# Query and key norm of a two-layer block: one chain of sums, roots and spread products made into two

## The reference

```
q = rms_norm(q, g_q) * (HEAD_DK ** -0.5)      # over each group of 64 channels
k = rms_norm(k, g_k)
bias = bias_table[t5_buckets(kpos[None, :] - qpos[:, None])]    # [q, k, head]
s = einsum('bqhjd,bkhjd->bhjqk', q, k) + bias
...
mod = dot(silu(c), w_mod) + b_mod              # shift1, scale1, gate1, shift2, scale2, gate2
x  = x + gate1 * mix
h2 = rms_norm(x, g_norm2) * (1.0 + scale2) + shift2
```

## Time and profile before

| | |
|---|---|
| median of 3 executions | 2403.66 us (2400.92 to 2405.05) |
| the profiled execution | 2396.91 us |
| its span in the trace | 2394.8 us |
| the block of the change | from 303.4 to 387.1 us of the span |
| PE busy | 2146.2 us (90% of the span) |
| DVE busy | 1744.9 us (73%) |
| ACT busy | 1053.7 us (44%) |
| POOL busy | 165.0 us (7%) |

### The profile page before, as it was taken

The page is one execution under the profiler, slowest core; times in us unless marked ns, Lnnn a source line. Parts: engine busy times, 40 slices in busy tenths (PEclk is TensorE's granted clock), DMA queues, the critical chain, the costliest instruction groups (busy, mean ns, idle before and its releaser), DMA issues. The chain is left out here.

```text
span 2394.8 us, 25614 instructions
## 1 busy us (share of the span) xinstructions
PE 2146.2 (90%) x10172; PEld 1667.9 (70%) x10172; DVE 1744.9 (73%) x1857; ACT 1053.7 (44%) x1190; POOL 165.0 (7%) x122
## 2 busy tenths in 40 slices
PE   5999979999954999999999069999999969899997
PEld 3767824667843888888887047888888647788775
DVE  4565135997467799999997359999999469955737
ACT  4387022774224677777775022112221246522123
POOL 2000000000000011111110000000000000042210
PEclk8999986999976999999999569999999978899999
DMA  9111170001276899999997311121222140332201
GB/s 316 44 36 36 36 286 0 1 1 72 88 277 254 316 403 394 395 393 403 393 393 245 127 44 38 63 79 36 83 102 88 33 153 1 124 114 88 71 1 71
DMA packets 125719, 365.03 MB, mean 152 GB/s; under 512 B 11733, under 2 KB 22893, under 8 KB 125623
## 3 DMA queue, kind: packets, MB, share of 16 engines
q1 hardware_dynamic: 111616, 328.68, 36.1%
q0 software_dynamic: 6336, 21.00, 3.4%
q10 hardware_dynamic: 7670, 14.03, 1.6%
HBM read 324.76 MB, written 38.86 MB: 152 GB/s over the span
## 5 line engine op out<-in xcount | busy, mean ns | idle before, releaser
L2031 DVE SCALAR_TENSOR_TENSOR arena<-arena,vecs 128x1023 f32<-128x1023 f32 (+14 forms) x240 | 304.4, 1268 | 7.1
L1560 DVE TENSOR_TENSOR w_low<-W,w_high 128x2048 fp32r<-128x2048 f32 x96 | 217.0, 2287 | 38.9 <-ACT w_high L1512 38.9
L1928 PE MATMUL Q<-hT_high,w_high 128*128 128x512 f32 (+1 forms) x736 | 227.0, 391 | 5.9 <-DVE ring_low L2074 5.8
L1560 DVE TENSOR_TENSOR w_low<-arena,w_high 128x2048 fp32r<-128x2048 f32 x96 | 218.3, 2290 | 17.7 <-ACT w_high L1512 17.7
L1512 ACT ACTIVATE w_high<-W 128x2048 fp32r<-128x2048 f32 x96 | 184.0, 1919 | 96.6 <-PE Q L1455 65.3
L1928 PE MATMUL Q<-hT_low,w_high 128*128 128x512 f32 (+1 forms) x720 | 222.2, 390 | 0.0
L1928 PE MATMUL Q<-hT_high,ring_low 128*128 128x512 f32 x704 | 217.2, 390 | 0.0
L1512 ACT ACTIVATE w_high<-arena 128x2048 fp32r<-128x2048 f32 x96 | 184.2, 1919 | 74.9 <-PE Q L1455 74.9
L1455 PE MATMUL Q<-w_high,x_high 128*128 128x512 f32 x512 | 160.8, 395 | 2.4 <-DVE x_low L1563 2.4
L1928 PEld LDWEIGHTS Q<-hT_high,w_high 128*128 128x128 f32 (+1 forms) x736 | 135.4, 184 | 39.0 <-DVE ring_low L2074 5.9
L1455 PE MATMUL Q<-w_low,x_high 128*128 128x512 f32 x512 | 158.8, 391 | 0.0
(11 more groups left out here) (430 smaller groups left out, 4295.1 us busy)
## 6 DMA issues: line engine op xcount, KB each, us to landing
W<-in_w_dram SPq DMA_DIRECT2D x48, 2048.0 KB, 13.3
arena<-in_w_dram SPq DMA_DIRECT2D x48, 2048.0 KB, 12.3
W<-in_w_mod_dram SPq DMA_DIRECT2D x12, 2048.0 KB, 9.5
W<-in_w_in_dram SPq DMA_DIRECT2D x12, 2048.0 KB, 8.7
W<-in_w_out_dram SPq DMA_DIRECT2D x6, 2048.0 KB, 9.0
spill<-arena ACTq DMA_DIRECT2D x24, 512.0 KB, 2.6
W<-in_w_in_dram SPq DMA_DIRECT2D x8, 1024.0 KB, 7.7
arena<-in_x_dram SPq DMA_DIRECT2D x4, 1024.0 KB, 17.4
```

The source lines that it names most:

```text
L1560: nc.vector.tensor_tensor(wl[:], chunk_src(r, j), wh[:].bitcast(F32), ALU.subtract).then_inc(low_v, 1)
L1928: ins = nc.tensor.matmul(Q[rows, 2 * (n % 4) + half, :], w[:, k], x[:, k, HALF * half:HALF * half + HALF], start=k == 0 and w is high and ...
L2031: ins = nc.vector.scalar_tensor_tensor(conf[:, i, j:], u[:, 0:S - j], w, conf[:, i, j:], ALU.mult, ALU.add)
```

## The change

- The norm is two chains, q (tiles 0 to 3) and k (tiles 4 to 7). Each has its 8 sums in its own rows (partitions 0 to 7 and 64 to 71) and PSUM pair, its own root, inversion and spread. The q chain's root and inversion stand in the lists between the sums of k.
- The inverse roots are split: ACT rounds them into rows 0 to 7 (64 to 71) of `qk_parts`, DVE puts the rest into rows 32 to 39 (96 to 103), the rows between are zero. `qk_spread` has the 0/1 matrix in both groups of rows, so one fp32r product over 40 rows spreads both parts. The spread uses two PSUM pairs in turn instead of four.
- `near` stands behind the first two sums and the first modulation vector. The bias transfers go from SP's list to POOL's; the weight units on SP follow the b_mod rows directly.
- The subtraction for the recurrent branch (`y_rest`, two instructions) goes to the end of DVE's list; the `gain2` load and the (1 + scale2) * g_norm2 step go to the output projection's block.

The diff, cut to its core:

```diff
-        VECS = 2 * 8
-        qk_sum = tiles(5)[:, 0:8 * VECS].rearrange("p (b r) -> p b r", b=8)
-        qk_spread = tiles(4)[0:VECS].rearrange("r (b p) -> r b p", b=8)
...
+        VECS = 2 * HEADS
+        qk_sum = tiles(5)[:, 0:HEADS * VECS].rearrange("p (b r) -> p b r", b=HEADS)
+        spread_whole = tiles(4)[:, 0:HALF]
+        qk_spread = rounded("qk_spread", 4, [P, 2, HEADS, P])[:, 1]
+        qk_parts = rounded("qk_parts", 3, [P, S])
+        sum_bank = (6, 2)
+        def rows_of(g):
+            return slice(DK * g, DK * g + VECS)
+        def rest_of(g):
+            return slice(DK * g + 32, DK * g + 32 + VECS)
...
-                sync.dma_start(gain2, bc_row(A["g_norm2"][0], D)).then_inc(gain2_in, 16)
...
-                for h in range(HEADS):
-                    sync.wait_ge(near_ready, h + 1)
-                    sync.dma_start(bias_rows[h].rearrange("(p n) -> p n", p=P), bias_near[h]).then_inc(bias_sent, 16)
-                sync.wait_ge(bias_sent, 16 * HEADS)
...
+                nc.gpsimd.memset(qk_parts[:].bitcast(F32), 0.0).then_inc(masks, 1)
+                for h in range(HEADS):
+                    pool.wait_ge(near_ready, h + 1)
+                    pool.dma_start(bias_rows[h].rearrange("(p n) -> p n", p=P), bias_near[h]).then_inc(bias_sent, 16)
+                pool.wait_ge(bias_sent, 16 * HEADS)
+                for h in range(HEADS):
+                    skewed = bias_rows[h, P:].rearrange("(p n) -> p n", n=HALF - 1)[:, 0:NEAR]
+                    pool.dma_start(bias_all[:, h, 6 * P:6 * P + NEAR], skewed).then_inc(bias_in, 16)
+                pool.wait_ge(bias_in, 16 * HEADS)
...
+                def next_vector(i):
+                    row_product(i)
+                    if i < 5:
+                        mod_product(pe, unit(pe, U_GATE1 + i + 1), 5)
+                def sums(g):
+                    for b in range(HEADS):
+                        n = HEADS * g + b
+                        pe.wait_ge(sq_ready, n + 1)
+                        for half in range(2):
+                            ins = nc.tensor.matmul(Q[rows_of(g), sum_bank[g] + half, :], qk_sum[:, b],
+                                                   tiles(n % 2)[:, HALF * half:HALF * half + HALF],
+                                                   start=b == 0, stop=b == HEADS - 1)
+                        ins.then_inc(sum_mm, 1)
+                        if b % 2:
+                            next_vector(2 * g + b // 2)
+                        if n == 1:
+                            near()
...
+                def spread(g):
+                    pe.wait_ge(parts_low, g + 1)
+                    span = slice(DK * g, DK * g + 32 + VECS)
+                    for b in range(HEADS):
+                        n = HEADS * g + b
+                        if n >= 2:
+                            pe.wait_ge(qk_normed, n - 1)
+                        for half in range(2):
+                            ins = nc.tensor.matmul(Q[:, 6 * (n % 2) + half, :], qk_spread[span, b],
+                                                   qk_parts[span, HALF * half:HALF * half + HALF],
+                                                   start=True, stop=True)
+                        ins.then_inc(spread_mm, 1)
...
                 mod_product(pe, unit(pe, U_GATE1), 5)
...
+                pe.wait_ge(masks, 2)
+                sums(0)
+                pe.wait_ge(near_ready, HEADS)
+                sums(1)
+                next_vector(4)
...
+                spread(0)
...
+                spread(1)
...
+                square(0)
+                square(1)
+                act.wait_ge(lam_mm, 1)
+                nc.scalar.activation(lam_pr[:, 2:4], Q[:, 4, 0:2], ACT.Exp).then_inc(lam_e, 1)
+                part(0)
+                square(2)
+                square(3)
+                act.wait_ge(masks, 6)
+                nc.scalar.activation(qk_spread, spread_whole.rearrange("r (b p) -> r b p", b=HEADS), ACT.Copy)\
+                    .then_inc(mask_ready, 1)
+                part(1)
+                root(0)
+                square(4)
+                square(5)
+                part(2)
+                square(6)
+                square(7)
+                act.wait_ge(masks, 7)
+                high_rows(0)
+                part(3)
+                root(1)
+                part(4)
...
+                part(5)
+                high_rows(1)
...
+                def invert(g):
+                    dve.wait_ge(root_q, g + 1)
+                    nc.vector.reciprocal(qk_rows[rows_of(g)], qk_rows[rows_of(g)]).then_inc(rows_inv, 1)
+                def low_rows(g):
+                    dve.wait_ge(parts_high, g + 1)
+                    nc.vector.tensor_tensor(qk_parts[rest_of(g)], qk_rows[rows_of(g)],
+                                            qk_parts[rows_of(g)].bitcast(F32), ALU.subtract).then_inc(parts_low, 1)
+                def norm(n):
+                    dve.wait_ge(spread_mm, n + 1)
+                    nc.vector.scalar_tensor_tensor(qk[:, n], qk[:, n], qk_gain[:, n // HEADS:n // HEADS + 1],
+                                                   bank2(3 * (n % 2)), ALU.mult, ALU.mult).then_inc(qk_normed, 1)
...
+                added(0)
+                for h in range(HEADS):
+                    dve.wait_ge(near_mm, h + 1)
+                    nc.vector.tensor_copy(bias_near[h], Q[:, h, :]).then_inc(near_ready, 1)
+                added(1)
+                invert(0)
+                added(2)
+                low_rows(0)
+                dve.wait_ge(near_ready, HEADS)
+                for h in range(HEADS):
+                    nc.vector.tensor_copy(bias_all[:, h, 0:6 * P], bias_near[h][:, 0:1].broadcast_to((P, 6 * P)))
+                    nc.vector.tensor_copy(bias_all[:, h, 6 * P + NEAR:],
+                                          bias_near[h][:, HALF - 1:HALF].broadcast_to((P, 6 * P)))
+                invert(1)
+                added(3)
+                added(4)
+                norm(0)
+                norm(1)
+                low_rows(1)
+                norm(2)
+                norm(3)
+                added(5)
+                for n in range(HEADS, 2 * HEADS):
+                    norm(n)
...
+                sync.dma_start(gain2, bc_row(A["g_norm2"][0], D)).then_inc(gain2_in, 16)
...
+                dve.wait_ge(gain2_in, 16)
+                nc.vector.scalar_tensor_tensor(SCALE2, SCALE2, 1.0, gain2, ALU.add, ALU.mult).then_inc(scale_made, 1)
```

More of the change, by code:

```diff
@@ L277, in program @@
         mod_rows = {4: GATE1, 6: SHIFT2, 8: SCALE2, 10: GATE2}
-        gain2 = tiles(3)
+        gain2 = tiles(2)
         GROUPS = 4
@@ L845, in row_product @@
                     nc.tensor.matmul(Q[:, 4, :], group_row, part_sb, start=True, stop=True).then_inc(row_mm, 1)
-                pe.wait_ge(masks, 3)
-                mod_product(pe, unit(pe, U_GATE1), 5)
-                for b in range(8):
-                    pe.wait_ge(sq_ready, b + 1)
-                    for half in range(2):
-                        ins = nc.tensor.matmul(Q[0:VECS, 6 + half, :], qk_sum[:, b],
-                                               tiles(b % 2)[:, HALF * half:HALF * half + HALF],
-                                               start=b == 0, stop=b == 7)
-                    ins.then_inc(sum_mm, 1)
-                    if b % 2:
-                        row_product(b // 2)
-                        mod_product(pe, unit(pe, U_GATE1 + b // 2 + 1), 5)
@@ new lines, in near @@
+                def near():
+                    pe.wait_ge(hot_in, 16)
+                    pe.wait_ge(table_ready, 1)
+                    for h in range(HEADS):
+                        nc.tensor.matmul(Q[:, h, :], table_bc[:, h], hot, start=True, stop=True).then_inc(near_mm, 1)
+                mod_product(pe, unit(pe, U_GATE1), 5)
+                pe.wait_ge(lam_ready, 1)
+                nc.tensor.matmul(Q[:, 4, 0:2], ones[0:DK, :], lam_pr[0:DK, 0:2], start=True, stop=True)\
+                    .then_inc(lam_mm, 1)
@@ L890, in _, with square, root @@
-                act.wait_ge(near_mm, HEADS)
+                def square(n):
+                    if n >= 2:
+                        act.wait_ge(sum_mm, n - 1)
+                    nc.scalar.activation(tiles(n % 2), qk[:, n], ACT.Square).then_inc(sq_ready, 1)
+                def root(g):
+                    act.wait_ge(sum_mm, HEADS * (g + 1))
+                    nc.scalar.activation(qk_rows[rows_of(g)],
+                                         Q[rows_of(g), sum_bank[g]:sum_bank[g] + 2, :].rearrange("p a b -> p (a b)"),
+                                         ACT.Sqrt, bias=eps_col[rows_of(g)], scale=1.0 / DK).then_inc(root_q, 1)
@@ new lines, in high_rows @@
+                def high_rows(g):
+                    act.wait_ge(rows_inv, g + 1)
+                    nc.scalar.activation(qk_parts[rows_of(g)], qk_rows[rows_of(g)], ACT.Copy).then_inc(parts_high, 1)
+                square(0)
[6 more added lines that the diff above has]
```

(8 more changed lines are left out.)

71 lines of the change are left out of this document (16 added, 55 removed).

## The result

| | median (executions) | range |
|---|---|---|
| before | 2403.12 us (4) | 2400.92 to 2405.05 |
| changed | 2376.90 us (4) | 2373.94 to 2381.78 |

The ratio is 0.9893, with a 95% interval of 0.9874 to 0.9912, so 26.2 us less. The forecast was 2382.5 us with a range of 2374.5 to 2390.0. The direction and the range held, and the gain was 5 us larger than the 21 of the forecast.

What follows compares the result with a forecast made beforehand. The block was taken as a serial piece of 83.7 us that nothing covers. Ending at 365.2 instead of 387.1 gives -21.9, the scale step +1.1, say -21: 2382.5 us from median 2403.66, range 2374.5 to 2390.0.

Steps and rivals of the forecast that it cites:

- The front: Block's start to the end of the eighth sum: work starts at 303.4 without waiting for one_hot, a gain of 9.8 us.
- T8: End of the eighth sum on PE in the block: 344.8 before, forecast 335, between 331.5 and 337.4.
- Root and fills: After the eighth sum, k's root takes 1.10 plus 0.3 to 336.4; q's fills end at 335.8, just hidden.
- The new gap on PE: PE idles some 5 us before row_product(4), waiting for added(3); low clock then: row product 1.9, modulation product 3.5.
- The first spread pair: First two rounded spread products after the modulation product: 0.9 plus 0.4 until DVE sees it, 1.3 us, to 350.3.
- DVE's row of norms to the end: Norms, low_rows, added(5) and subtractions on DVE, 13.9 us plus 1.0 of stalls, ending the block at 365.2.
- The tail: From the end of the eighth sum to the block's end: 42.3 us before, forecast 30.2.
- The moved scale step: (1 + scale2) * g_norm2, 1.23 us on DVE, delays the output projection's split and PE: charged at 1.1 us.
- the front gained more than forecast: Answers the first rival: late b_mod rows or a 1.2 GHz clock leave a gain of 15, 2389 us; chance 0.09.
- the spread is faster: Answers the second rival: fp32r products over 40 rows cost what float32 did, gain 4, 2400 us; chance 0.04.
- the bias chain on POOL: Third rival: POOL's bias transfers end the block last, at 377 if they take 60 us; gain 9, 2395; chance 0.03.
- the attention lost nothing: Answers the fourth rival: the clock stays down in the attention, 4.4 us lost a turn, eight turns 2418; chance 0.02.

Runs made afterwards that it cites:

- the two runs that began it at 2.4 GHz: Kernel before with its float32 spread over 128 rows, 2385.53 us; and the changed kernel with three steps moved plus nine unread float32 products, 2371.77 us.
- the one chain over 128 rows: Changed kernel with one 16-row norm chain, added(3) early, subtractions and scale step in DVE's gaps, rounded spread over 128 rows: 2371.01 us.
- the float32 spread: Changed kernel with plain float32 spread products over the 8 rows of a chain, without rounding or rest: 2390.49 us, block 69.9 us.
- the three moved steps run again: Changed kernel with added(3) before the second inversion, and subtractions and scale step in DVE's waits; second timing 2370.16 us, block 51.4 us.

## Why the prediction was right, and where it was off

Its steps, each by its own numbers:

- **The front.** Forecast T8 31.6 us after the start of the block, measured 30.2 (332.58 + 3.60 - 306.02). The b_mod rows landed 12.6 us after the start, as taken. What was off is the clock. It was taken half down over the front; the trace has 0.93. Near ran at full clock (3.88) and the price came one step later, in the sums behind it (5.07 instead of 3.60). The lower bound of 28.1 (T8 = 331.5) was not reached.
- **Root and fills.** The second inversion was to start within 2 us of T8 + 1; it started 1.8 after T8. The fills ended 0.7 us after the root: hidden, but only just.
- **The second inversion** is not hidden and takes 6.54, as forecast 6.53.
- **The new gap on PE**: forecast some 5 us, measured 6.34. The products behind it were taken at the low clock (1.9 and 3.5). The row product was low (2.05), but the clock came back in the modulation product (2.56).
- **The first spread pair**: 1.3 forecast until DVE starts, 0.8 measured (349.89 to 350.66), since it met the full clock. The bounds had been 0.5 and 3.4 for a pair; 4 products over 40 rows take 1.21 at 2.4 GHz and 2.41 at 1.2 GHz (those of k, 0.50 in their stretch), always under the 2.5 of two norms.
- **DVE's row of norms to the end**: 14.9 forecast with stalls of 1.0, 14.1 measured (350.66 to 364.73). The stalls did not come: the four norms of k take 5.05 us without a wait, though their spread products ran at 1.2 GHz. The tail from T8 is 28.5 instead of 30.2.
- **The moved scale step**: charged at 1.1, it cost 0.45 in the length of the stage. The timeline of the output projection shows it:

```profile
594.63 1.22 DVE L1398 SCALAR_TENSOR_TENSOR arena<-arena 128x1024 f32<-128x1024 f32 x1
595.77 2.49 DVE L1053 TENSOR_TENSOR ring_low<-W,ring_low 128x512 fp32r<-128x512 f32 x4
...
596.51 0.50 PE L1233 MATMUL Q<-ring_low,att_high 128*128 128x512 f32 x1 [0.53 <-DVE ring_low L1053]
```

Of the 1.22 us, PE waits 0.53 for the split, and no later wait adds to it. Moved into a wait of DVE it costs nothing (115.3 for the stage).

In sum 1.4 us of the front, 1.7 of the tail and 0.65 of the moved step explain 3.8 of the 5 us between forecast and result; the rest is within what executions of the untouched parts differ by. The largest mis-sized term is TensorE's clock, which was taken too low in three places: 1.4 us in the front, 0.8 in the two products before the spread, 0.5 in the first pair. The stalls that did not come give 0.8 more and the moved step 0.65; only the second inversion came later than forecast, by 0.5. That the block ended at 364.73 where 365.2 was forecast is chance, since it also began 2.6 us later; its length to the last work of DVE is 58.7 us, not 61.8. Two slips in the prediction's side sums change nothing: 317 and 30 us make 347, not 349, and the upper bound's gain is 16.3, not 17.

The rivals: the front gained more than forecast; the spread is faster (undoing it costs 10.5 us); the bias chain on POOL ended early (below); and the attention lost nothing, because it began at the low clock before as well.

Three steps of the forecast named what the change leaves lying: that halving the rows gains nothing in the inversion, that PE idles for added(3), and that the subtractions now come last. The runs gave each its price: about 1 us or nothing for two chains, 4.9 for the order, and 2 to 3 for the subtractions in the block, with 0.8 more in the output projection for the scale step (116.1 to 115.3).

**The bias transfers.** The landing times (KB each, median us) by queue, to be set against the earlier trace rows:

```profile
bias_rows<-arena POOLq DMA_DIRECT2D x4, 256.0 KB, 6.2
arena<-bias_rows POOLq DMA_DIRECT2D x4, 192.0 KB, 6.6
```

The stores take 6.2 us instead of 2.5, and the loads 6.6 instead of 2.8. Two things changed for them at once, the queue and the weight units that now run beside them; back on SP with the units behind them they take 2.2, and no run tells the two apart. They are issued at 320.25 and 329.22, so the chain is over near 338, long before 365.

## What to carry to other kernels

Where an engine's list has a step for which another engine waits, and a long one for which nobody waits yet, the step goes first; here this was worth 5 us, and the division into two chains about 1 us or nothing. Look at the granted clock of a product over few rows: here the spread ran at 1.2 GHz. Padding it with zero rows took it from 27.67 to 16.75 us where PE was busy throughout and did nothing for the clock where PE paused; using products of rounded values cut its price at the same clock. Before a transfer chain is taken to be harmless on a queue, look at what will stand behind it once the rest is faster.

## What the runs showed of the hardware

- An inversion of 8 x 1024 and one of 16 x 1024 cost the same 6.5 us, 6.4 ns for each element of one partition; one of 128 x 32, in the output projection of the kernel before, takes 0.35. So it is the elements of a partition that count, and not the rows. A norm over the same 1024 elements takes 1.26 us.
- The attention took 175.2 and 175.7 us in the two runs that began it at 2.4 GHz, and 177.5 to 180.5 in the others. Part of that range is how soon the clock came back: over its first 22 us the mean was 0.58 before (180.45 us), 0.67 and 0.90 in the two traces of the changed kernel (180.3 and 178.4), and 0.90 in the one chain over 128 rows (177.5). So a full clock at its start is worth some 2 to 5 us.
- What near cost in clock varied too: near and the sums behind it took 7.29 us in two traces (the float32 spread, and the three moved steps run again), 10.65 with the bias transfers on SP, and 8.9 to 9.0 in the others that have this order.
- VectorE's copies within SBUF held up GpSimd while it issued transfers, in the one place where the two met. The prediction named this rule of the Trainium skill (DMA: Bandwidth & Descriptors, SWDGE vs HWDGE vs iDMA) and put 3.8 us on it. In the changed kernel the two never met: its four loads were issued in 2.13 us beside the inversion. In the float32 run the fills came early and met them:

```profile
328.18 5.79 POOL L842 DMA_DIRECT2D arena<-bias_rows  x4 [6.63 <-DMA bias_rows<-arena]
...
329.50 0.54 DVE L999 COPY arena<-arena 128x768 f32<-128x768 f32 x1
...
332.78 0.54 DVE L1000 COPY arena<-arena 128x768 f32<-128x768 f32 x1
```

Eight copies from 329.50 to 333.32 fall into the four issues, which take 5.79 us instead of 2.13, 3.7 more, and the last is issued at 333.4, when the copies have ended. The copies themselves keep their 0.54. The trace agrees with the rule; copies from PSUM, beside which the stores were issued (2.32 for four), did not show it.
